# The square of the decay in the second half of a recurrent branch: on GpSimd instead of a second ScalarE exponential

## The chip, the cores and the metric

The kernel runs on one core of a Trainium2 chip. The metric is the device time of one launch in microseconds (us); three runs of the kernel before have a median of 1281.16 us. Engines are named as in the profile: PE (TensorE; PEld its weight loads), DVE (VectorE), ACT (ScalarE), POOL (GpSimd), SP (SyncE, which issues the DMAs here).

## The reference, cut to what matters

A two-layer backbone for 128 prompt and 256 sample tokens. In each layer a latent attention and a bidirectional linear recurrence (the branch) run side by side, are merged by gates, and a feed-forward block follows. The change touches the coefficients of the recurrence, which the reference computes for each of the 1024 channels in both directions as

```python
r = sigmoid(block_diag(x, w_rg) + b_rg)
i = sigmoid(block_diag(x, w_ig) + b_ig)
log_a = -8.0 * softplus(-lam) * r
a = exp(log_a)
u = sqrt(-expm1(2.0 * log_a)) * i * x
# h[t] = a[t] * h[t-1] + u[t]
```

The kernel takes sqrt(1 - a^2) as the square root of (1 + a^2) * tanh(-log_a).

## The kernel before, in words

All 384 tokens lie along the free dimension; 1024 channels are eight chunks of 128 partitions. A tile of one chunk is 128x384 in float32. Every large weight matrix comes in as loads of 128x1024 (`raw`, three buffers); ACT copies each to a rounded "high" half (`highs`, L1269) and DVE subtracts it to make the "low" half (`lows`, L1651); PE then does three products for each pair (L718 high with high, L725 high with low activations, L726 low with high). Five buffers of each half exist. The order of all work on each engine is written out by hand, and semaphores count the steps.

Each layer starts with jobs `lx0`, `lx1`, `qk`, `kr`, `gg0`, `gg1`, `m2a`, `m2b`, `m1a`, `m1b`: each is 1024x512 of weights, eight chunk steps of about 2.08 us on PE. While PE does `m2a` and `m2b`, ACT and DVE do the second group of the branch's coefficients (chunks 4 to 7, `b == 1`).

On ACT that is `lru_coefficients(1, ...)`: a table load, then for each (chunk c, direction d) one exponential of twice the argument into the scratch tile `t[d]` (L1445) and one in place for the decay `a` into `r_` (L1446). From the third pair on, the first of them waits for the DVE to be done with `t[d]`. After both directions of the next chunk are begun, `tau` of a chunk gets its logarithm (L1452) and exponential of half (L1454), both 128x768; the logarithm waits for the second direction's `squared_roots`. `highs` of the loads m2a 3, m2b 0, 1, 2 and 3 are woven in, and behind m2b 1 two reciprocal roots of the latent norms (L1360, L1363), which free the banks that `m2b` needs.

On DVE the order is: `squared_roots(4)` (L1960, `tau = (t + 1) * tau`, one 128x384 operation for each direction, each waiting for `a`), `lows` m2a 3, `squared_roots(5)`, `mod_result(6)` (small; only in layer 0), `scans(4)` (two products L1935, four scans L1939 and L1943, two tiny copies, a sum L1949), `lows` m2b 0, `squared_roots(6)`, `lows` m2b 1, `scans(5)`, `squared_roots(7)`, `lows` m2b 2, five products for the latents (L2038, L2042), `scans(6)`, `lows` m2b 3, then `lows` m1a 0, `scans(7)`.

On GpSimd, behind some memsets, the only work of a layer is the copies of rotated keys (L647, 32x512) and queries (L652, 32x128), the first of which waits for the step `cache` much later in the layer.

Of the kernel before, what the change touches and what calls it, by code (L numbers as in the profile page):

```python
# [23 lines left out]
C = D // P  # L24
# [12 lines left out]
ALU = mybir.AluOpType  # L37
ACT = mybir.ActivationFunctionType
# [166 lines left out]
def program(nc, A, plan):  # L205
# [3 lines left out]
    with ExitStack() as ctx:  # L209
        def sb(name, shape, dt=F):  # L210
            return ctx.enter_context(nc.sbuf_tensor(name, shape, dt))
# [59 lines left out]
        decay, ndecay, ndecay2 = lam[4], lam[5], lam[6]  # L271
# [5 lines left out]
        t = [sb(f"t{i}", [P, T]) for i in range(2)]  # L277
# [6 lines left out]
        def region(name, at, shape, dt=F):  # L284
            return nc.alloc_sbuf_tensor_at(name, shape, dt, offset=arena_at + at)
# [8 lines left out]
        r_ = region("lru_r", 12 * TB, [P, 2, 4, T])  # L294
# [36 lines left out]
        def qt(h):  # L331

            return qkv[:, h, :] if h < 6 else q_last[:, h - 6, :]

        def lru_under(h):

            return (keys_at + (h + 1) * TK * 4 - 1) // TB - 36
# [18 lines left out]
        PE, AC, VE, GP = tensor_done, scalar_done, vector_done, gpsimd_done  # L356
# [12 lines left out]
        def in_layer(l):  # L369


            def at(s, *label, prev=False):
                return s.sem, s.value(l - 1 if prev else l, *label)
            return at

        def last(l, s):

            return s.sem, s.count
# [29 lines left out]
        for name, reads in jobs:  # L408
            if name in HOSTED:
                reads.append((VE, "partial", HOSTED[name]))  # L410
            for r in [r for r, _, fold_job in MODS if fold_job == name]:
                reads.append((VE, "mod", r))
# [9 lines left out]
        def bank(job, b):  # L422
            return ps[4 * set_of[job] + b]
# [204 lines left out]
        @block.gpsimd  # L628
        def _(gp):
            nc.gpsimd.memset(ones[:, :], 1.0).then_inc(start_gp, 1)  # L630
            nc.gpsimd.memset(cs[:, :, :], 0.0).then_inc(start_gp, 1)
            nc.gpsimd.memset(epsc[:, 0:1], EPS).then_inc(start_gp, 1)
            nc.gpsimd.memset(epsc[:, 1:2], TINY).then_inc(start_gp, 1)
            nc.gpsimd.memset(one_row[:, 0:31], 0.0).then_inc(start_gp, 1)
            nc.gpsimd.memset(one_row[:, 31:32], 1.0).then_inc(start_gp, 1)
            nc.gpsimd.memset(one_row[:, 32:63], 0.0).then_inc(start_gp, 1)
            for s in (*raw_full, *mod_full, rows_full, gain_full, cache_full, stored):
                gp.sem_inc(s.sem, 1)
            gp.sem_inc(GP.sem, 1)
            for l in range(DEPTH):  # L640
                at = in_layer(l)
                GP.begin_layer(l)

                def key_turned(h):
                    if lru_under(h) >= 0:
                        gp.wait_ge(*at(VE, "lru_full", lru_under(h)))
                    nc.gpsimd.tensor_copy(kt[TURNED, h, :], kt[TURNED, 0, :]).then_inc(*GP.step("key_turned", h))  # L647

                def query_prompt(j):
                    gp.wait_ge(*at(AC, "qn", 3 * j + 2))  # L650
                    for e in range(4):
                        nc.gpsimd.tensor_copy(qt(4 * j + e)[TURNED, 0:TP], sq[2 + j][32 * e:32 * e + 32, 0:TP]  # L652
                                              ).then_inc(*GP.step("query_prompt", 4 * j + e))

                gp.wait_ge(*at(VE, "cache"))
                for h in range(1, 5):
                    key_turned(h)
                query_prompt(0)
                key_turned(5)
                query_prompt(1)  # L660
                key_turned(6)
                key_turned(7)
# [582 lines left out]
        def _(ac):  # L1245
# [7 lines left out]
            for l in range(DEPTH):  # L1253
                at = in_layer(l)
# [3 lines left out]
                def highs(job, i, ahead=0, layer=l):  # L1258

                    upto = layer * len(SPLIT) + SIDX[of_job(job)[i]] + ahead  # L1260
                    while made[0] <= upto:
                        lm, m = divmod(made[0], len(SPLIT))
                        n = SPLIT[m]
                        atm = in_layer(lm)
                        ac.wait_ge(*atm(raw_full[m % RAW], "load", n))

                        ac.wait_ge(*atm(PE, "used", SPLIT[m - SPL], prev=m < SPL))
                        for high, w in pieces(LOADS[n], wh[m % SPL], raw[m % RAW]):
                            nc.scalar.activation(high, w, ACT.Copy).then_inc(*AC.step())  # L1269
                        AC.also("high", n, layer=lm)  # L1270
                        made[0] += 1
# [86 lines left out]
                def inverse_root(which, src, n, dst=rstd):  # L1358

                    nc.scalar.activation(dst[:, :], src[:, 0:T], ACT.Ln, scale=1.0 / n, bias=epsc[:, 0:1]  # L1360
                                         ).then_inc(*AC.step("rs", which))
                    ac.wait_ge(*last(l, AC))
                    nc.scalar.activation(dst[:, :], dst[:, :], ACT.Exp, scale=-0.5).then_inc(*AC.step("rstd", which))  # L1363
# [68 lines left out]
                def lru_coefficients(b, after):  # L1432


                    nc.scalar.preload_act_table_set(EXP_LN)
                    ac.wait_ge(*last(l, AC))
                    order = [(j, d) for j in range(4) for d in range(2)]
                    for e in range(len(order) + 2):
                        if e < len(order):
                            j, d = order[e]  # L1440
                            c = 4 * b + j
                            k = C * d + c
                            if e >= 2:
                                ac.wait_ge(*at(VE, "squared_root", c - 1, d))
                            nc.scalar.activation(t[e % 2][:, :], r_[:, d, j, :], ACT.Exp, scale=ndecay2[:, k:k + 1]).then_inc(*AC.step())  # L1445
                            nc.scalar.activation(r_[:, d, j, :], r_[:, d, j, :], ACT.Exp, scale=ndecay[:, k:k + 1]  # L1446
                                                 ).then_inc(*AC.step("a", c, d))
                        if e >= 2 and e % 2 == 0:
                            j = e // 2 - 1
                            c = 4 * b + j  # L1450
                            ac.wait_ge(*at(VE, "squared_root", c, 1))
                            nc.scalar.activation(tau[:, :, j, :], tau[:, :, j, :], ACT.Ln, bias=epsc[:, 1:2]).then_inc(*AC.step())  # L1452
                            ac.wait_ge(*last(l, AC))
                            nc.scalar.activation(tau[:, :, j, :], tau[:, :, j, :], ACT.Exp, scale=0.5).then_inc(*AC.step("root", c))  # L1454
                        if e in after:
                            highs(*after[e])
                        if b == 0 and e in (2, 3):
                            latents(e + 2)
                        if b == 1 and e == 5:
                            ac.wait_ge(*at(PE, "latent_norms"))  # L1460
                            inverse_root("q", bank("st_qkv", 0), QL, sq[0])
                            inverse_root("kv", bank("st_qkv", 1), KVL, sq[1])

                def latents(c):

                    job, b = ("qk", c) if c < 4 else ("kr", c - 4)
                    ac.wait_ge(*at(PE, job, b))
                    if c < 5:
                        nc.scalar.activation(latent_sq[c], bank(job, b)[:, 0:T], ACT.Square).then_inc(*AC.step("sqq", c))
                    nc.scalar.activation(qkv[:, c, :], bank(job, b)[:, 0:T], ACT.Copy).then_inc(*AC.step("qkv", c))  # L1470
# [135 lines left out]
                for j in range(FC // 2):  # L1606
                    highs(f"fi{j}", -1, ahead=2)
                    for g in range(2):
                        c = 2 * j + g
# [4 lines left out]
                    for g in range(2):  # L1614
                        c = 2 * j + g
# [13 lines left out]
        def _(ve):  # L1629
# [4 lines left out]
            for l in range(DEPTH):  # L1634
                at = in_layer(l)
# [320 lines left out]

                def squared_roots(c):
                    for d in range(2):
                        ve.wait_ge(*at(AC, "a", c, d))
                        nc.vector.scalar_tensor_tensor(out=tau[:, d, c % 4, :], in0=t[d][:, :], scalar=1.0, in1=tau[:, d, c % 4, :],  # L1960
                                                       op0=ALU.add, op1=ALU.mult).then_inc(*VE.step("squared_root", c, d))

# [245 lines left out]
                for j in range(FC // 2):  # L2208
                    lows(f"fi{j}", -1, ahead=2)
                    for g in range(2):  # L2210
                        c = 2 * j + g
# [5 lines left out]
                    for g in range(2):  # L2217
                        c = 2 * j + g
# [71 lines left out]
```

## Time and profile before

| | |
|---|---|
| median of three runs (lowest, highest) | 1281.16 us (1281.06, 1282.22) |
| the profiled execution | 1280.97 us, of which the span is 1278.9 us |
| TensorE's mean granted clock | 0.997 of full speed |
| PE busy | 1242.3 us |
| DVE busy | 836.5 us |
| ACT busy | 658.0 us |
| POOL busy | 18.4 us |

The span runs from the first to the last instruction of the trace. A busy share is over the whole span and says little of a short stretch; the timeline of one engine lists its instructions with their start, duration and, in brackets, the idle time before them and what ended it. Neighbouring instructions of an engine overlap by some 0.1 us in it.

### The profile page before, as it was taken

The numbers are of one execution on the slowest core, as the hardware profiler recorded it, in microseconds if no ns is written. First come the engines' busy times: TensorE is split into PE (matmuls) and PEld (weight loads), VectorE is DVE, ScalarE is ACT, GpSimd is POOL, SyncE is SP. The second block draws the span as 40 slices with busy tenths as digits, with TensorE's granted clock in tenths as the row PEclk, the third lists the DMA queues.
The fourth block names the chain that finished last, engine by engine and source line by source line (L and its number), as shares of the span: only waits on it lengthen the run. The fifth ranks groups of instructions, "written<-read, shape, count | busy, mean of one in ns | idle before, by whom it ended". The sixth has DMA issues, their size and how long they took to land.

```text
span 1278.9 us, 19550 instructions
## 1 busy us (share of the span) xinstructions
PE 1242.3 (97%) x7457; PEld 1145.8 (90%) x7457; DVE 836.5 (65%) x1382; ACT 658.0 (51%) x1161; POOL 18.4 (1%) x41
## 2 busy tenths in 40 slices
PE   6999999999999999999999999999999999999998
PEld 4899999978879999998879998998798899999886
DVE  2697684764868877749768795756566884343423
ACT  5479873754454333342255989557445533333322
POOL 0000000200000000000000000011000000000000
PEclk9999999999999999999999999999999999999999
DMA  9645555333346766548824334263325464444451
GB/s 335 211 135 160 184 163 196 106 116 115 113 134 213 230 208 220 166 135 274 271 63 139 103 108 116 84 232 115 100 76 164 154 201 129 132 132 132 157 165 49
DMA packets 132128, 199.34 MB, mean 156 GB/s; under 512 B 10330, under 2 KB 70980, under 8 KB 132036
## 3 DMA queue, kind: packets, MB, share of 16 engines
q1 hardware_dynamic: 132036, 198.11, 48.7%
q8 instruction: 59, 0.97, 0.3%
q14 instruction: 33, 0.27, 0.1%
HBM read 196.16 MB, written 1.92 MB: 155 GB/s over the span
## 4 chain that ended last, share of the span: by engine, by line
PE 78%; DVE 10%; ACT 7%; issue 2%; DMA 1%; SPq 1%; DVEq 0%; ACTq 0%
PE bank L718 16%; PE bank L725 16%; PE bank L726 16%; PE bank L837 6%; PE bank L838 6%; PE bank L839 6%; DVE weight_low L1651 3%; ACT weight_high L1269 2%; ACT sq L1277 1%; PE bank L1137 1%; DVE lru_h L1939 1%; PE bank L1161 1%; DVE lru_tau L1943 1%; PE bank L755 1%; DVE lru_i L1935 1%
## 5 line engine op out<-in xcount | busy, mean ns | idle before, releaser
L725 PE MATMUL bank<-act_low,weight_high 128*128 128x384 f32 x1440 | 487.7, 339 | 3.6 <-DVE weight_low L1651 3.6
L726 PE MATMUL bank<-act_high,weight_low 128*128 128x384 f32 x1440 | 482.6, 335 | 0.0
L1651 DVE TENSOR_TENSOR weight_low<-raw,weight_high 128x1024 fp32r<-128x1024 f32 (+5 forms) x282 | 319.8, 1152 | 168.8 <-ACT weight_high L1269 168.4
L1269 ACT ACTIVATE weight_high<-raw 128x1024 fp32r<-128x1024 f32 (+5 forms) x282 | 273.0, 995 | 224.7 <-DMA raw<-in_w_ffn_out 62.5
L718 PE MATMUL bank<-act_high,weight_high 128*128 128x384 f32 x1440 | 315.1, 339 | 4.4 <-ACT sq L1360 2.7
L725 PEld LDWEIGHTS bank<-act_low,weight_high 128*128 128x128 f32 x1440 | 271.3, 188 | 10.9 <-DVE weight_low L1651 5.8
L726 PEld LDWEIGHTS bank<-act_high,weight_low 128*128 128x128 f32 x1440 | 271.3, 188 | 0.0
L718 PEld LDWEIGHTS bank<-act_high,weight_high 128*128 128x128 f32 x1440 | 253.6, 188 | 12.0 <-issue 4.7
L837 PE MATMUL bank<-weight_high,hid_high 128*128 128x512 f32 x264 | 103.2, 391 | 0.0
L839 PE MATMUL bank<-weight_high,hid_low 128*128 128x512 f32 x264 | 102.8, 389 | 0.0
L838 PE MATMUL bank<-weight_low,hid_high 128*128 128x512 f32 x264 | 102.8, 389 | 0.0
L1613 ACT ACTIVATE sq<-bank 128x384 f32<-128x384 f32 x44 | 19.2, 489 | 141.1 <-PE bank L726 141.1
L2215 DVE TENSOR_TENSOR t<-bank,sq 128x384 f32<-128x384 f32 x44 | 24.5, 558 | 97.2 <-PE bank L726 93.7
L837 PEld LDWEIGHTS bank<-weight_high,hid_high 128*128 128x128 f32 x264 | 49.6, 188 | 10.9 <-issue 0.6
L839 PEld LDWEIGHTS bank<-weight_high,hid_low 128*128 128x128 f32 x264 | 49.5, 188 | 10.3
L838 PEld LDWEIGHTS bank<-weight_low,hid_high 128*128 128x128 f32 x264 | 49.6, 188 | 10.1
L1675 DVE SCALAR_TENSOR_TENSOR qkv<-mod_weight,cs,qkv 128x1024 f32<-128x1024 f32 x42 | 52.0, 1279 | 1.9 <-DMA mod_weight<-in_w_mod 1.9
L1567 ACT ACTIVATE sq<-bank 128x384 f32<-128x384 f32 (+1 forms) x48 | 20.2, 421 | 55.4 <-PE bank L1146 28.2
L2156 DVE TENSOR_REDUCE negmax<-bank 128x1 f32<-128x384 f32 (+1 forms) x48 | 22.1, 464 | 31.5 <-PE bank L1137 31.3
L837 PE MATMUL bank<-weight_high,act_high 128*128 128x512 f32 x96 | 37.6, 392 | 0.0
L838 PE MATMUL bank<-weight_low,act_high 128*128 128x512 f32 x96 | 37.4, 390 | 0.0
L839 PE MATMUL bank<-weight_high,act_low 128*128 128x512 f32 x96 | 37.4, 390 | 0.0
(262 smaller groups left out, 1473.3 us busy)
## 6 DMA issues: line engine op xcount, KB each, us to landing
raw<-in_w_ffn_in SPq DMA_DIRECT2D x176, 256.0 KB, 3.9
mod_weight<-in_w_mod SPq DMA_DIRECT2D x80, 512.0 KB, 4.8
raw<-in_w_in SPq DMA_DIRECT2D x72, 512.0 KB, 4.0
raw<-in_w_ffn_out SPq DMA_DIRECT2D x44, 512.0 KB, 4.5
first_mod<-in_w_mod SPq DMA_DIRECT2D x4, 2048.0 KB, 14.2
raw<-in_w_o_lru SPq DMA_DIRECT2D x16, 512.0 KB, 3.7
raw<-in_w_out SPq DMA_DIRECT2D x16, 512.0 KB, 3.7
raw<-in_w_o_mla SPq DMA_DIRECT2D x8, 512.0 KB, 5.0
```

The costliest lines, as they stand in the source:

```text
L718: nc.tensor.matmul(bank(job, g)[:, 0:T], view[0][:, kk, cols], high[:, k, :], start=k == 0, stop=False)
L725: nc.tensor.matmul(o, view[0][:, kk, cols], low[:, k, :], start=False, stop=False)
L726: ins = nc.tensor.matmul(o, view[1][:, kk, cols], high[:, k, :], start=False, stop=k == total - 1)
L837: nc.tensor.matmul(o, high[:, k, toks], view[0][:, kk, :], start=k == 0, stop=False)
L838: nc.tensor.matmul(o, high[:, k, toks], view[1][:, kk, :], start=False, stop=False)
L839: ins = nc.tensor.matmul(o, low[:, k, toks], view[0][:, kk, :], start=False, stop=k == 2 * pairs - 1)
L1269: nc.scalar.activation(high, w, ACT.Copy).then_inc(*AC.step())
L1567: nc.scalar.activation(sq[2 + s % 2][:, 0:n * P], bank("attn", 2)[:, 0:n * P], ACT.Copy).then_inc(*AC.step("pt", s))
L1651: nc.vector.tensor_tensor(low, w, high.bitcast(F), ALU.subtract).then_inc(*VE.step())
L1675: nc.vector.scalar_tensor_tensor(out=total(r, g), in0=w, scalar=c, in1=total(r, g), op0=ALU.mult, op1=ALU.add).then_inc(*VE.step())
L2156: nc.vector.tensor_reduce(negmax[:, s % 2:s % 2 + 1], bank("attn", s % 2)[:, 0:n], AX.X, ALU.max, negate=True).then_inc(*VE.step("max", s))
L2215: nc.vector.tensor_tensor(t[c % 2][:, :], bank(f"fi{j}", 2 + g)[:, 0:T], sq[c % 4][:, :], ALU.mult).then_inc(*VE.step("hid", c))
```

## The change

For chunks 4 to 7 the exponential of twice the argument (L1445) is no longer issued on ACT, and with it goes ACT's wait for `squared_root` of the chunk before. GpSimd computes `t[d] = a * a` instead: one 128x384 product, both inputs the same tile of `r_`, for each chunk and direction, eight for a layer. It waits for `a` and, from chunk 5 on, for the DVE's reading of `t[d]` of the chunk before. DVE's `squared_roots` waits for GpSimd's product in place of ACT's `a`. The new loop stands ahead of GpSimd's key copies. Chunks 0 to 3 are as before.

```diff
@@ gpsimd, ahead of the wait for "cache"
+                for c in range(4, C):
+                    for d in range(2):
+                        if c > 4:
+                            gp.wait_ge(*at(VE, "squared_root", c - 1, d))
+                        gp.wait_ge(*at(AC, "a", c, d))
+                        nc.gpsimd.tensor_tensor(t[d][:, :], r_[:, d, c % 4, :], r_[:, d, c % 4, :], ALU.mult
+                                                ).then_inc(*GP.step("squared", c, d))
@@ scalar, lru_coefficients
-                            if e >= 2:
-                                ac.wait_ge(*at(VE, "squared_root", c - 1, d))
-                            nc.scalar.activation(t[e % 2][:, :], r_[:, d, j, :], ACT.Exp, scale=ndecay2[:, k:k + 1]).then_inc(*AC.step())
+                            if b == 0:
+                                if e >= 2:
+                                    ac.wait_ge(*at(VE, "squared_root", c - 1, d))
+                                nc.scalar.activation(t[e % 2][:, :], r_[:, d, j, :], ACT.Exp, scale=ndecay2[:, k:k + 1]).then_inc(*AC.step())
@@ vector, squared_roots
-                        ve.wait_ge(*at(AC, "a", c, d))
+                        ve.wait_ge(*(at(AC, "a", c, d) if c < 4 else at(GP, "squared", c, d)))
```

## Rows read from the trace of the kernel before

**Rows 1.** The page: busy time of PE, and the chain that ended last by engine.
```profile
PE 1242.3 (97%) x7457; PEld 1145.8 (90%) x7457; DVE 836.5 (65%) x1382; ACT 658.0 (51%) x1161; POOL 18.4 (1%) x41
...
PE 78%; DVE 10%; ACT 7%; issue 2%; DMA 1%; SPq 1%; DVEq 0%; ACTq 0%
```

**Rows 2.** Timeline of PE: end of m2a and job m2b of layer 0, then m2b of layer 1.
```profile
166.51 0.34 PE L725 MATMUL bank<-act_low,weight_high 128*128 128x384 f32 x1
...
170.45 0.97 PE L718 MATMUL bank<-act_high,weight_high 128*128 128x384 f32 x4 [0.30 <-ACT sq L1360]
...
179.58 0.33 PE L725 MATMUL bank<-act_low,weight_high 128*128 128x384 f32 x1
...
185.01 0.44 PE L725 MATMUL bank<-act_low,weight_high 128*128 128x384 f32 x1 [1.11 <-DVE weight_low L1651]
...
811.18 0.44 PE L725 MATMUL bank<-act_low,weight_high 128*128 128x384 f32 x1 [0.65 <-DVE weight_low L1651]
```

**Rows 3.** Busy time by stretch, layer 0 and 1: PE, PEld, DVE, ACT, POOL, clock, DMA.
```profile
163.30:185.00 21.70, 20.30 (x141) 19.22 (x139) 21.34 (x47) 18.82 (x28) 0.00 (x0) 1.00 0.47 141
...
789.90:811.20 21.30, 18.25 (x105) 17.61 (x103) 20.97 (x42) 18.82 (x28) 0.00 (x0) 1.00 0.29 84
```

**Rows 4.** Timeline of DVE, the second group of layer 0.
```profile
158.63 0.56 DVE L1960 SCALAR_TENSOR_TENSOR lru_tau<-t,lru_tau 128x384 f32<-128x384 f32 x1 [0.46 <-ACT lru_r L1446]
159.58 1.23 DVE L1651 TENSOR_TENSOR weight_low<-raw,weight_high 128x1024 fp32r<-128x1024 f32 x1 [0.39 <-ACT weight_high L1269]
...
163.31 0.56 DVE L1960 SCALAR_TENSOR_TENSOR lru_tau<-t,lru_tau 128x384 f32<-128x384 f32 x1 [2.04 <-ACT lru_r L1446]
163.79 0.38 DVE L1714 TENSOR_REDUCE mod<-bank 128x2 f32<-128x8 f32 x4
164.20 0.17 DVE L1718 TENSOR_TENSOR mod<-mod,par 128x8 f32<-128x8 f32 x1
...
176.12 1.22 DVE L1651 TENSOR_TENSOR weight_low<-raw,weight_high 128x1024 fp32r<-128x1024 f32 x1
...
183.74 1.22 DVE L1651 TENSOR_TENSOR weight_low<-raw,weight_high 128x1024 fp32r<-128x1024 f32 x1
```

**Rows 5.** Timeline of ACT, the same stretch.
```profile
156.46 0.62 ACT L1445 ACTIVATE t<-lru_r,lam 128x384 f32<-128x384 f32 x1
156.99 0.60 ACT L1446 ACTIVATE lru_r<-lru_r,lam 128x384 f32<-128x384 f32 x1
...
160.47 0.93 ACT L1452 ACTIVATE lru_tau<-lru_tau,epsc 128x768 f32<-128x768 f32 x1
...
162.18 0.60 ACT L1445 ACTIVATE t<-lru_r,lam 128x384 f32<-128x384 f32 x1
162.68 0.60 ACT L1446 ACTIVATE lru_r<-lru_r,lam 128x384 f32<-128x384 f32 x1
163.19 1.05 ACT L1269 ACTIVATE weight_high<-raw 128x1024 fp32r<-128x1024 f32 x1
```

**Rows 6.** Timeline of POOL, layer 0: key and query copies.
```profile
207.68 0.60 POOL L647 COPY keys<-keys 32x512 f32<-32x512 f32 x1 [206.27 <-DVE keys L2080]
...
235.06 0.88 POOL L647 COPY keys<-keys 32x512 f32<-32x512 f32 x1 [2.45 <-DVE t L2118]
...
243.28 0.84 POOL L652 COPY q_last<-sq 32x128 f32<-32x128 f32 x2
```

**Rows 7.** Timeline of DVE around those copies.
```profile
234.91 0.55 DVE L2100 TENSOR_TENSOR act_low<-t,act_high 128x384 fp32r<-128x384 f32 x1
235.38 1.10 DVE L1651 TENSOR_TENSOR weight_low<-raw,weight_high 128x512 fp32r<-128x512 f32 x1
236.41 0.68 DVE L1651 TENSOR_TENSOR weight_low<-raw,weight_high 128x512 fp32r<-128x512 f32 x1
...
242.66 1.76 DVE L2113 TENSOR_TENSOR qkv<-sq 32x256 f32<-32x256 f32 x4
```

## The prediction

> **What bounds the kernel now.** I read the page first: PE is busy 97% of the span and holds 78% of the chain that ended last; DVE has 10% and ACT 7% of it [rows 1]. So a change on ACT, DVE and POOL moves the time only where PE waits for them. The timeline of PE over the second group of coefficients shows where: in job m2b of layer 0 PE stands 1.11 us, and in layer 1 0.65 us, until the low half of the last load, m2b 3, is made by DVE [rows 2]. Behind these two points PE runs on, so what this low half gains or loses is the gain or loss of the layer. The 0.30 us at the start of m2b, which ACT ends, is no bound of its own: PE would only reach the later stall sooner.
>
> The timeline of DVE says what sets that low half. It starts at 183.74; DVE last stood idle for long (2.04 us) before the second L1960 of chunk 5, at 163.31, waiting for ACT's decay [rows 4]. From there on it is busy 21.34 of 21.70 us in layer 0 and 20.97 of 21.30 us in layer 1 [rows 3]. So the time at which PE goes on is: the start of that L1960, plus the DVE work behind it, plus whatever disturbs DVE on the way. ACT, which the change relieves, matters up to 163.3 and then no more; POOL, which it loads, is empty in both stretches (0.00) [rows 3].
>
> **What is removed.** Eight exponentials of 0.60 us, which lie about 0.51 us apart, for a layer [rows 5]: 4.1 us of ACT. Four of them stand ahead of the decay that DVE awaits at 163.31 (chunk 4 and 5, both directions): 4 x 0.51 = 2.0 us at most. The other four come while DVE is the bound and are worth nothing. ACT's wait for `squared_root` goes too; the logarithm L1452 keeps its own, on the second direction of the same chunk.
>
> **What is added, the product itself.** The trace shows no two-input operation on POOL. The nearest row is its 32x512 copy: 0.60 us undisturbed [rows 6]. How long it keeps the memory reads shows from a collision, below: 0.42 us for 512 elements, 0.82 ns each, so about 0.2 us of the copy is fixed. For 384 elements one pass is 0.32 us, two (both inputs one after the other) are 0.64, three (and the write) are 0.96. Bounds for the hold H: 0.32 to 0.96 us. I take 0.80, between two and three passes, since a product has one input more than the copy and must write as well. The product lasts G = H + 0.2 = 1.0 us (0.5 to 1.16). GPSIMD Engine Reference of the Trainium skill (3.1, elementwise cycle accounting) gives 4497 ns for a two-input operation of 2048 elements, 2.2 ns an element, an estimate of 0.84 us for H; the sum below would come out 0.6 us higher.
>
> **What is added, the collision.** At 235.06 POOL starts a copy while DVE runs L2100 (234.91 to 235.46). The copy takes 0.88 in place of 0.60 us: it waits. The next DVE instruction, L1651 at 235.38, takes 1.10 us where the one behind it, of the same shape, takes 0.68: it waits 0.42 [rows 6, 7]. So the two shut each other out instruction by instruction, and a POOL operation that is waiting gets in ahead of DVE's next. Four L2113 at 242.66 fit this: they span 1.76 us instead of 1.44 (0.42 each, 0.34 apart), 0.11 us more for each step, which is what 128 elements cost at 0.82 ns [rows 7]. SBUF — State Buffer of the Trainium skill (Who interferes with whom) says that a DVE instruction with two SBUF inputs and a GpSimd one that reads SBUF block each other fully; by that rule, too, the products cost DVE their whole hold, and the collision at 235.4 agrees.
>
> Nearly everything DVE does in the bound run has two SBUF inputs: L1651, L1935, L1960, the scans, L1949, L2038. So a product that falls into it costs DVE about H, though POOL itself has nothing else to do.
>
> **The start of the run, step by step (layer 0).** The first decay is now where the first exponential was: out at 156.46 + 0.62 = 157.1. Products 4,0 and 4,1 follow: 157.1 + G, then H + 0.1 more, 159.0 (case G = 1.0). DVE is shut out or behind, so both its L1960 of chunk 4 come after: 0.05 + 0.47 + 0.56, done at 160.1, where they were done at 159.2 [rows 4]. L1452 waits for that; from its start to the end of the decay of (5,1) were 160.47 to 163.28 us with an exponential of 0.51 in between, so 2.3 us now [rows 5]: 162.4. Then product 5,1: 0.05 + G, and 0.05 to DVE: 163.5, against 163.31. In H: 161.14 + 3H, that is 163.54 at 0.80 and 163.06 and 164.02 at 0.64 and 0.96. Three products in series eat the 2 us of ACT: **+0.2 us** (-0.3 to +0.7). Waiting behind these on DVE is everything, low halves included, but that of m2a 3 ends at 160.8 and PE wants it at 166.51, 5.7 us later [rows 2, 4]. Layer 1 repeats these steps without a difference that matters. DMAs, SP and the key copies of POOL (207.7) are far behind and touch nothing.
>
> **The four products inside the run** (chunks 6 and 7). Product 6,0 needs its decay, out on ACT about 163.9 (162.4, then a high half of 1.0 and itself 0.5 [rows 5]); DVE then has 5,1 behind it. In layer 0 it meets the small reductions from PSUM (163.79 to 164.2, one input), which hide about 0.4 us [rows 4]; layer 1 has none. Product 6,1 falls in scans(4), 7,0 behind the first L1960 of chunk 6, 7,1 in scans(5). Each waits for one DVE instruction and then holds the next back by H. There is no idle time of DVE to take them in: 21.70 - 21.34 us is 0.4, all of it short gaps.
>
> Layer 0: 0.2 + 4 x 0.8 - 0.4 = +3.0. Layer 1: 0.2 + 3.2 = +3.4. What is late next: low m2b 2 would end at 177.3 + 3 = 180.3, and PE wants it at 179.58 [rows 2, 4], so PE stands there first and then again at m2b 3; the sum stays that of the last. ACT's relief (rs earlier, the 0.30 us gone) only makes PE arrive at the stall sooner. PE then has no slack later that would take it back, as job follows job and it is the bound. Profiled 1280.97 + 6.4 = **1287.4 us**; the median before lies 0.2 above the profiled execution, inside the precision of this sum. With H of 0.64 the sum is 4.2 (1285.2), with 0.96 it is 8.7 (1289.7).
>
> **Rivals.**
> A. No shutting out that matters (DVE wins the port in its gaps, or a square of one tile reads cheaply). Then only the start moves: 157.7 + 2G + 2.4 + G = 160.1 + 3G, against 163.31. With G = 1.0 that is -0.2 us a layer: 1280.6, no change. For it: POOL copies of 128 elements pass beside DVE with 0.11 us each. Against it: the 0.42 us at 235.38.
> B. The same with a fast product, G = 0.52 (one pass): 161.7, -1.6 us a layer, 1277.7. This is the other side, faster, and its turning point is G = 1.07 without collisions. With collisions and one pass the start gains 1.2 and four holds of 0.32 give it back: -0.3 and +0.1 us, 1280.7.
> C. The scans do not shut POOL out (no row shows the two beside each other): products 6,1 and 7,1 are free, 1.6 us less a layer: 1284.2.
> D. A price at the first product of a kind on POOL. The first key copy takes 0.60 us like the others [rows 6], which speaks against it; if there were 6 us at 157.1 in layer 0, DVE would start its run that much later: 1293. The GPSIMD Engine Reference (2.1, dispatch) names about 6 us for the first call to freshly loaded code, and no row here shows one.
>
> **How the numbers follow.** Forecast 0.57 (1285.2 to 1289.7). C 0.16. A, with the one-pass variant with collisions, 0.16. B 0.05. D or other double costs 0.06. Range: 1280.2 takes in A and C; 1290.5 is the forecast's end with some room; B and D stay out. A measurement of this kernel can tell about 0.2% (2.6 us) from no change. Faster by more: B, 0.05. Within: A and a third of a C with smaller holds, 0.20. Slower: the forecast, most of C, and D, 0.75.
>
> **What would show it.** Right: POOL products of 0.9 to 1.4 us, the longer ones where they wait; DVE instructions beside them 0.6 to 0.9 us longer than their kind; the second L1960 of chunk 5 still near 163.3 to 164; low m2b 3 at about 186.7 and PE's stall before it near 3 to 4 us in all, with one at m2b 2. Wrong: DVE's forms as long as before and a start at 161 to 163 (A, B); only L1935, L1949 and L1651 stretched and the scans not (C); a long gap before the first product (D). If PE's later stalls shrink by what these grow, the bound was misread.

## The result and the profile after

The changed kernel takes 1289.68 us in the median (1287.17 to 1290.4, five runs), the kernel before beside it 1282.22 us: 1.0061 times as long, 95% interval 1.005 to 1.0072. A second set of five runs on another chip gave 1288.74 against 1280.79 us, 1.0065 (1.0052 to 1.0077). The profiled execution took 1287.17 us, 6.2 us more than that of before; its span is 1285.4 us, 6.5 us more. Two single runs of experiments, of 4754.6 and 5834.21 us, are left out of the medians below.

The page of the changed kernel, its busy line:

```profile
PE 1246.1 (97%) x7457; PEld 1149.4 (89%) x7457; DVE 843.7 (66%) x1382; ACT 650.8 (51%) x1145; POOL 33.4 (3%) x57
```

Against [rows 1], ACT has 16 instructions and 7.2 us less, POOL 16 instructions and 15.0 us more; and DVE, whose instructions are the same 1382, is busy 7.2 us longer. PE's stalls in m2b, which answer to [rows 2]:

```profile
180.99 0.44 PE L732 MATMUL bank<-act_low,weight_high 128*128 128x384 f32 x1 [0.16 <-DVE weight_low L1659]
188.61 0.45 PE L732 MATMUL bank<-act_low,weight_high 128*128 128x384 f32 x1 [3.17 <-DVE weight_low L1659]
...
807.84 0.45 PE L732 MATMUL bank<-act_low,weight_high 128*128 128x384 f32 x1 [0.53 <-DVE weight_low L1659]
815.46 0.69 PE L732 MATMUL bank<-act_low,weight_high 128*128 128x384 f32 x1 [3.18 <-DVE weight_low L1659]
```

PE now stands 3.17 and 3.18 us where it stood 1.11 and 0.65 (the load m2b 3), and shortly once more one load earlier (m2b 2), as the prediction had it. (The lines of code moved: L1651 is L1659, L1960 is L1968, L1935 is L1943, L1939 and L1943 are L1947 and L1951, L1949 is L1957, L1446 is L1454, L1435 is L1442, L725 is L732, L1718 is L1726.) DVE over the same stretch of layer 0, answering to [rows 4]:

```profile
159.65 1.63 DVE L1968 SCALAR_TENSOR_TENSOR lru_tau<-t,lru_tau 128x384 f32<-128x384 f32 x2 [1.89 <-POOL t L660]
...
162.97 0.55 DVE L1968 SCALAR_TENSOR_TENSOR lru_tau<-t,lru_tau 128x384 f32<-128x384 f32 x1
164.64 0.56 DVE L1968 SCALAR_TENSOR_TENSOR lru_tau<-t,lru_tau 128x384 f32<-128x384 f32 x1 [1.12 <-POOL t L660]
165.12 0.38 DVE L1722 TENSOR_REDUCE mod<-bank 128x2 f32<-128x8 f32 x4
165.53 0.72 DVE L1726 TENSOR_TENSOR mod<-mod,par 128x8 f32<-128x8 f32 x1
...
168.21 0.98 DVE L1951 TENSOR_TENSOR_SCAN lru_tau<-lru_r,lru_i 128x128 f32<-128x128 f32 x1
...
172.67 1.85 DVE L1659 TENSOR_TENSOR weight_low<-raw,weight_high 128x1024 fp32r<-128x1024 f32 x1
...
175.49 0.93 DVE L1947 TENSOR_TENSOR_SCAN lru_h<-lru_r,lru_i 128x128 f32<-128x128 f32 x1
```

And POOL beside it:

```profile
163.78 0.83 POOL L660 TENSOR_TENSOR t<-lru_r 128x384 f32<-128x384 f32 x1 [1.81 <-ACT lru_r L1454]
165.40 0.83 POOL L660 TENSOR_TENSOR t<-lru_r 128x384 f32<-128x384 f32 x1 [0.79 <-DVE mod L1722]
167.70 1.22 POOL L660 TENSOR_TENSOR t<-lru_r 128x384 f32<-128x384 f32 x1 [1.47 <-DVE lru_h L1947]
172.36 1.07 POOL L660 TENSOR_TENSOR t<-lru_r 128x384 f32<-128x384 f32 x1 [3.45 <-DVE lru_tau L1968]
175.25 0.89 POOL L660 TENSOR_TENSOR t<-lru_r 128x384 f32<-128x384 f32 x1 [1.81 <-ACT lru_r L1454]
```

An undisturbed product takes 0.83 us. The last four of a layer lie in DVE's run, and each has one stretched DVE instruction beside it: L1726 0.72 in place of 0.17 us, a scan of 128 elements 0.98 in place of 0.40, L1659 1.85 in place of 1.22, a scan 0.93 in place of 0.42. That is 0.55 + 0.58 + 0.63 + 0.51 = 2.27 us. In layer 1 the same four products lengthen these:

```profile
792.35 1.65 DVE L1943 TENSOR_TENSOR lru_i<-lru_i,lru_tau 128x384 f32<-128x384 f32 x2
...
795.02 1.03 DVE L1951 TENSOR_TENSOR_SCAN lru_tau<-lru_r,lru_i 128x128 f32<-128x128 f32 x1
...
799.52 1.85 DVE L1659 TENSOR_TENSOR weight_low<-raw,weight_high 128x1024 fp32r<-128x1024 f32 x1
...
802.34 0.93 DVE L1947 TENSOR_TENSOR_SCAN lru_h<-lru_r,lru_i 128x128 f32<-128x128 f32 x1
```

Against 1.02, 0.40, 1.22 and 0.42 us in the kernel before that is 0.63 + 0.63 + 0.63 + 0.51 = 2.40 us.

To compare kernels without what happens elsewhere in an execution, I read one length in each trace and layer: from ACT's table load that opens the second group to the instant at which PE goes on with m2b 3. In the kernel before these table loads are

```profile
155.17 1.28 ACT L1435 ACT_TABLE_LOAD   x1
...
781.77 1.28 ACT L1435 ACT_TABLE_LOAD   x1
```

so with 185.01 and 811.18 [rows 2] the lengths are 29.84 and 29.41 us. In the changed kernel:

```profile
156.80 1.28 ACT L1442 ACT_TABLE_LOAD   x1
...
784.02 1.28 ACT L1442 ACT_TABLE_LOAD   x1
```

31.81 and 31.44 us: +1.97 and +2.03. The start of DVE's run moved from 8.14 to 7.84 us behind the table load (163.31 - 155.17, 164.64 - 156.80), -0.30; with the 2.27 us of stretched instructions that makes the 1.97 of layer 0. In layer 1 it moved by as much (789.92 - 781.77 is 8.15, 791.87 - 784.02 is 7.85), and 2.40 - 0.30 is 2.10 against 2.03 measured.

Both layers together give 4.0 us, but the kernel is 6 to 8 us slower. A part of the rest is in the granted clock. These are stretches of layer 1 in and behind the stall (PE, PEld, DVE, ACT, POOL busy, the clock, DMA):

```profile
812.00:815.00 3.00, 0.28 (x2) 0.00 (x0) 2.93 (x7) 1.34 (x3) 0.00 (x0) 1.00 0.00 0
815.00:818.00 3.00, 2.54 (x8) 2.54 (x9) 2.97 (x6) 0.00 (x0) 0.00 (x0) 0.51 0.45 106
818.00:821.00 3.00, 3.00 (x18) 3.00 (x17) 2.31 (x6) 0.59 (x2) 0.00 (x0) 0.92 0.71 245
```

After 3.18 us without a matmul PE runs at 0.51 (1.2 in place of 2.4 GHz), which costs at most 0.49 x 3 + 0.08 x 3 = 1.7 us; some 0.2 us of that fall in the last 0.46 us of the stall, where PE still stood. Behind the 3.17 us of layer 0 the clock stayed at 1.00 in this execution. The mean granted clock of the five runs is 0.991 to 0.994, that of before's profile 0.997, and the two runs at 0.994 (1287.17, 1287.83) are about 2 us shorter than the three at 0.991 and 0.992. The runs of before beside the experiments lie between 0.994 and 0.999.

The stall of layer 1 did not grow by lateness alone. The start of m2b there, before and after:

```profile
797.06 0.98 PE L718 MATMUL bank<-act_high,weight_high 128*128 128x384 f32 x4 [2.40 <-ACT sq L1360]
...
797.29 0.97 PE L725 MATMUL bank<-act_high,weight_high 128*128 128x384 f32 x4 [0.38 <-ACT sq L1367]
```

Before, PE stood 2.40 us here for ACT and the granted clock stayed at 1.00. With ACT relieved it stands 0.38 us, and a part of the idle time moves to the one stall at m2b 3: from 0.65 to 3.18 us, and 0.53 at m2b 2, where the low half came 2.03 us later.

### The profile page after: what moved, and what is told of

Read it like the earlier page. It is cut to its first block, busy times and chain, and to the rows that moved or that the text cites. A ratio compares the mean times of both kernels' runs of the same rounds, so it can differ in the third digit from the quotient of the medians.

```text
span 1285.4 us, 19564 instructions
## 1 busy us (share of the span) xinstructions
PE 1246.1 (97%) x7457; PEld 1149.4 (89%) x7457; DVE 843.7 (66%) x1382; ACT 650.8 (51%) x1145; POOL 33.4 (3%) x57
## 3 DMA queue, kind: packets, MB, share of 16 engines
HBM read 196.16 MB, written 1.92 MB: 154 GB/s over the span
## 4 chain that ended last, share of the span: by engine, by line
PE 79%; DVE 10%; ACT 5%; issue 2%; DMA 2%; SPq 0%; DVEq 0%; POOL 0%; ACTq 0%
PE bank L725 17%; PE bank L732 16%; PE bank L733 16%; PE bank L844 5%; PE bank L845 5%; PE bank L846 5%; DVE weight_low L1659 3%; ACT weight_high L1276 1%; PE bank L1144 1%; DVE lru_h L1947 1%; PE bank L1168 1%; PE bank L762 1%; ACT sq L1284 1%; DVE lru_tau L1951 1%; DVE lru_i L1943 1%
## 5 line engine op out<-in xcount | busy, mean ns | idle before, releaser
L732 PE MATMUL bank<-act_low,weight_high 128*128 128x384 f32 x1440 | 489.1, 340 | 9.4 <-DVE weight_low L1659 9.4
L1659 DVE TENSOR_TENSOR weight_low<-raw,weight_high 128x1024 fp32r<-128x1024 f32 (+5 forms) x282 | 322.2, 1161 | 171.0 <-ACT weight_high L1276 170.5
L725 PE MATMUL bank<-act_high,weight_high 128*128 128x384 f32 x1440 | 315.6, 339 | 2.0 <-ACT act_high L1361 1.2
L732 PEld LDWEIGHTS bank<-act_low,weight_high 128*128 128x128 f32 x1440 | 272.2, 189 | 17.3 <-DVE weight_low L1659 12.2
L725 PEld LDWEIGHTS bank<-act_high,weight_high 128*128 128x128 f32 x1440 | 254.5, 189 | 9.2 <-issue 3.9
```

The costliest lines, as they stand in the source:

```text
L725: nc.tensor.matmul(bank(job, g)[:, 0:T], view[0][:, kk, cols], high[:, k, :], start=k == 0, stop=False)
L732: nc.tensor.matmul(o, view[0][:, kk, cols], low[:, k, :], start=False, stop=False)
L1659: nc.vector.tensor_tensor(low, w, high.bitcast(F), ALU.subtract).then_inc(*VE.step())
```

## The experiments

Each ran beside the kernel before on the same chip. Theory 1: a GpSimd product that reads memory and a VectorE instruction shut each other out, and what lengthens the run is these holds. Theory 2, the rival: the loss is VectorE waiting at its semaphores for slow products.

**Products beside, unused.** The kernel before, with the eight products added into a free tile that nobody waits for before the region is reused. Cut from the excerpt: GpSimd first waits until the tile is free, and ACT waits for the last product behind its wait for the scans of chunk 7.

```diff
+                for c in range(4, C):
+                    for d in range(2):
+                        if c > 4:
+                            gp.wait_ge(*at(VE, "squared_root", c - 1, d))
+                        gp.wait_ge(*at(AC, "a", c, d))
+                        gp.wait_ge(GP.sem, GP.count)
+                        nc.gpsimd.tensor_tensor(rstd[:, :], r_[:, d, c % 4, :], r_[:, d, c % 4, :], ALU.mult
+                                                ).then_inc(*GP.step("squared", c, d))
```

> The kernel before, unchanged on ScalarE and VectorE, with the eight GpSimd products of each layer added beside it; they write a spare tile that nobody reads. Theory 1 (each product that reads memory shuts VectorE out for its hold, 0.63 us as the changed kernel's trace shows, and the reverse): the run of VectorE ends later by 4 to 5 holds in each layer, 2 to 3 us, so 4 to 6 us in all, 1286 to 1288 us, though nothing waits for GpSimd. Theory 2 (the loss of the changed kernel is VectorE's waiting for slow products at its semaphores): no change, within 1 us.

Measured: 1287.67 against 1281.39 us, 1.0052 (1.0039 to 1.0065). The lengths are 32.19 and 32.18 us, +2.35 and +2.77. DVE in layer 0 (here L1946 is L1935 of before, L1950 and L1954 are L1939 and L1943, L1960 is L1949):

```profile
164.19 0.38 DVE L1729 TENSOR_TENSOR mod<-mod,par 128x8 f32<-128x8 f32 x1
...
165.54 0.93 DVE L1950 TENSOR_TENSOR_SCAN lru_h<-lru_r,lru_i 128x128 f32<-128x128 f32 x1
...
168.35 0.96 DVE L1960 TENSOR_TENSOR lru_h<-lru_h,lru_tau 128x384 f32<-128x384 f32 x1
...
172.45 1.65 DVE L1946 TENSOR_TENSOR lru_i<-lru_i,lru_tau 128x384 f32<-128x384 f32 x2
...
175.12 0.98 DVE L1954 TENSOR_TENSOR_SCAN lru_tau<-lru_r,lru_i 128x128 f32<-128x128 f32 x1
```

DVE never waits for these products, and the loss is as large as with the change. The run starts where it did (163.30 against 163.31), and, ACT not being relieved, five products fall into it: 0.21 + 0.51 + 0.40 + 0.63 + 0.58 = 2.33 us of stretched instructions, against +2.35 measured. Theory 2 falls.

**No square at all.**

```diff
-                        nc.vector.scalar_tensor_tensor(out=tau[:, d, c % 4, :], in0=t[d][:, :], scalar=1.0, in1=tau[:, d, c % 4, :],
+                        nc.vector.scalar_tensor_tensor(out=tau[:, d, c % 4, :], in0=t[d][:, :] if c < 4 else r_[:, d, c % 4, :], scalar=1.0, in1=tau[:, d, c % 4, :],
```

with the GpSimd loop left out and ACT as in the change.

> The second group without any square: ScalarE issues only the eight decays, GpSimd does nothing, VectorE reads the decay itself where it read the square. Left out of the computation: the square in chunks 4 to 7. This is the relief of ScalarE alone. Worked out from the timeline: the second VectorE L1960 of chunk 5 starts at 161.3 in place of 163.3, so 2.0 us less in each layer, 4 us in all, 1278 us. A theory by which VectorE is the bound all along and ScalarE's relief is worth nothing gives no change.

Measured: 1275.12 against 1281.39 us, 0.9954 (0.9942 to 0.9967). In layer 1 PE goes on at 805.84, 27.32 us behind the table load at 778.52: -2.09, as the timeline of before gave. In layer 0 PE does not stand at m2b 3 at all: it starts that product at 183.29, 27.92 us behind the table load at 155.37 (-1.92), and the low half was ready at 183.13. So ACT's relief is worth about 2 us a layer when the square is free, 4.0 us in all. The other 2 us of the difference are not in this stretch.

**Chunks 4 and 5 alone, chunks 6 and 7 alone.** In the three places of the change:

```diff
-                for c in range(4, C):
+                for c in range(4, 6):
...
-                            if b == 0:
+                            if not 4 <= c < 6:
...
-                        ve.wait_ge(*(at(AC, "a", c, d) if c < 4 else at(GP, "squared", c, d)))
+                        ve.wait_ge(*(at(AC, "a", c, d) if not 4 <= c < 6 else at(GP, "squared", c, d)))
```

and the same with 6 and 8.

> The change for chunks 4 and 5 alone; 6 and 7 keep ScalarE's second exponential. Theory 1: the run of VectorE starts 0.3 us sooner in each layer and no product falls into it: 0 to 1 us less than before. Theory 2 (waiting for products): chunks 4 and 5 are the ones whose products VectorE waits for, so here is the whole loss, 6 us more than before.

> The change for chunks 6 and 7 alone; 4 and 5 keep ScalarE's second exponential. Theory 1: four products shut VectorE out for 0.63 us each in its bound run, less some 0.4 us in layer 0: 2.1 and 2.5 us, 4.6 us more in all, and perhaps 1 to 2 us on top where a longer stall of TensorE is followed by a stretch at the lower clock. Theory 2: VectorE never waits for these products, so no change.

Measured for 4 and 5: 1280.79 against 1281.39 us, 0.9995 (0.9986 to 1.0004), lengths 29.55 and 29.05, -0.29 and -0.36. For 6 and 7: 1287.66 us, 1.0043 (1.0031 to 1.0056), lengths 32.08 and 31.21, +2.24 and +1.80. The products of chunks 4 and 5, which DVE waits for, cost nothing; those of chunks 6 and 7 are the whole loss. Layer 1 came out 0.7 us under the 2.5 expected, and the timeline of DVE there shows where from:

```profile
794.49 1.25 DVE L1947 TENSOR_TENSOR_SCAN lru_h<-lru_r,par,lru_i 128x256 f32<-128x256 f32 x1
...
796.73 0.15 DVE L1954 COPY hst<-lru_h 128x1 f32<-128x1 f32 x1
796.80 0.14 DVE L1955 COPY hst<-lru_tau 128x1 f32<-128x1 f32 x1
796.98 0.76 DVE L1957 TENSOR_TENSOR lru_h<-lru_h,lru_tau 128x384 f32<-128x384 f32 x1
```

One product fell beside the two tiny copies, which have one input each, and held back the sum behind them by 0.20 us only (L1957, 0.76 for 0.56); the other three cost 0.5 to 0.6 us each.

**One input in place of two.**

```diff
-                        nc.gpsimd.tensor_tensor(t[d][:, :], r_[:, d, c % 4, :], r_[:, d, c % 4, :], ALU.mult
+                        nc.gpsimd.tensor_copy(t[d][:, :], r_[:, d, c % 4, :]
```

> The changed kernel with a GpSimd copy of the decay, one input, in place of the product, in all eight places; left out of the computation: the square in chunks 4 to 7. If the hold goes by passes over the memory (0.82 ns an element and input), GpSimd's instruction is 0.52 us, VectorE's stretched instructions are 0.32 us longer and not 0.63, the start of the run comes 1.2 us earlier than before the change, and the layer is even: within 1 us of before. If each GpSimd instruction has a fixed price whatever it reads, it is as slow as the changed kernel.

Measured: 1282.33 against 1280.79 us, 1.001 (0.9997 to 1.0023); lengths 29.27 and 29.20, -0.57 and -0.21. POOL and DVE in layer 1:

```profile
789.58 0.51 POOL L660 COPY t<-lru_r 128x384 f32<-128x384 f32 x1 [0.98 <-ACT lru_r L1454]
...
790.60 1.35 DVE L1943 TENSOR_TENSOR lru_i<-lru_i,lru_tau 128x384 f32<-128x384 f32 x2
...
793.28 1.01 DVE L1951 TENSOR_TENSOR_SCAN lru_tau<-lru_r,par,lru_i 128x256 f32<-128x256 f32 x1
...
797.13 1.52 DVE L1659 TENSOR_TENSOR weight_low<-raw,weight_high 128x1024 fp32r<-128x1024 f32 x1
```

The copy takes 0.51 us and stretches DVE by 0.33 (1.35 for 1.02), 0.29 (1.01 for 0.72) and 0.30 (1.52 for 1.22): half of the product's 0.63. The fourth of this layer costs 0.20 (0.93 for 0.73). So the hold fits one price for each input read, about 0.32 us for 384 elements; a copy and a product differ in the operation too, and no run holds the two apart.

**The changed kernel again, and TensorE kept busy in its stall.** Theory 3: the idle stretch costs a second time through the lower clock. Theory 4: these falls come by chance.

```diff
                             if kk == 0:
+                                if job == "m2b" and i == 3:
+                                    for f in range(24):
+                                        nc.tensor.matmul(bank(job, f % 4)[:, T:512], ident[:, :], ident[:, :], start=False, stop=False,
+                                                         skip_group_check=True)
                                 pe.wait_ge(*at(VE, "low", n))
```

> The changed kernel once more, on the chip of the three runs beside it: 6 to 9 us more than before. In its first profile TensorE's stall of 3.18 us in layer 1 was followed by some 3.4 us at half of the granted clock, the one of 3.17 us in layer 0 was not; where both are, it is nearer to 9, where none, to 5.

> The changed kernel with 24 small matmuls on TensorE (identity with identity, into unused columns of the same banks) ahead of the wait for the last low half of m2b; they fill some 2.6 us of the 3.2 us stall and nobody reads them. Theory 3 (the idle stretch costs a second time, by the lower clock that follows it): the granted clock stays full behind the stall in both layers and the kernel is 1.7 to 3.4 us faster than the changed one, 4 to 5 us above before. Theory 4 (the clock's falls come by chance and owe nothing to this stall): the same time as the changed kernel, and a fall there as often as in it.

Measured: the changed kernel 1288.74 us, 8.0 us over before, with a fall of the clock at both stalls of its profiled execution; with 24 small matmuls 1289.25 us: no difference, as theory 4 says. But the timeline of PE shows why:

```profile
185.39 5.52 PE L729 MATMUL bank<-ident 128*128 128x128 f32 x48
190.67 0.42 PE L736 MATMUL bank<-act_low,weight_high 128*128 128x384 f32 x1
```

They took 5.5 us, not 2.6 (I had counted half of them: each is two in the trace), and the layer was 1.8 us longer than the changed kernel's, 190.67 - 157.08 = 33.59. The clock had not fallen at m2b in either layer, so one price may hide the other. Half as many tell them apart:

> As the run with 24 small matmuls, with 12 of them: the 24 took 5.5 us, 2 us more than the stall, and the fall of the granted clock was absent in both layers, so one hid the other. Theory 3: 12 take 2.8 us, fit in the 3.2 us, and the kernel is 1.7 to 3.4 us faster than the changed kernel, 1285 to 1287 us. Theory 4: it stays where the changed kernel is, 1289 us.

```profile
183.80 2.73 PE L729 MATMUL bank<-ident 128*128 128x128 f32 x23
187.04 0.44 PE L736 MATMUL bank<-act_low,weight_high 128*128 128x384 f32 x1 [0.51 <-DVE weight_low L1663]
```

```profile
812.00:815.00 3.00, 3.00 (x27) 3.00 (x26) 2.93 (x8) 1.76 (x4) 0.00 (x0) 1.00 0.00 0
815.00:818.00 3.00, 2.50 (x16) 2.31 (x15) 2.97 (x5) 0.00 (x0) 0.00 (x0) 1.00 0.34 55
```

Measured: 1285.88 against 1281.15 us, 1.0036 (1.0022 to 1.005), where the changed kernel had 1.0061 and 1.0065. The small matmuls take 2.7 us (the rows above leave out the first of 24). The lengths are the changed kernel's, 31.80 and 31.45, and the clock stays at 1.00. So about 3 us of the loss is the clock at the two stalls (3.2 and 3.7 us by the two ratios of the changed kernel; the intervals, 1.005 to 1.0072 and 1.0052 to 1.0077, lie just above that of this run). Over all traces with a stall of 2.8 to 3.2 us there, the clock fell at 9 of 11 stalls, in eight of them up to 1.2 us before PE went on, once 0.7 us behind; with the small matmuls at 0 of 4. The two exceptions are layer 0 of the first profile and the 3.10 us of layer 1 in the run with one input.

**All products on VectorE.**

```diff
+                    if c >= 4:
+                        for d in range(2):
+                            if c > 4:
+                                ve.wait_ge(*at(VE, "squared_root", c - 1, d))
+                            ve.wait_ge(*at(AC, "a", c, d))
+                            nc.vector.tensor_tensor(t[d][:, :], r_[:, d, c % 4, :], r_[:, d, c % 4, :], ALU.mult).then_inc(*VE.step())
                     for d in range(2):
```

> The changed kernel with all eight products of a layer on VectorE itself, in pairs, GpSimd left out. Each costs VectorE about 0.47 us of its own time, less than the 0.63 us for which a GpSimd product shuts it out. The start of the run comes 0.8 us earlier, four products in it cost 1.9 us: 1.1 us more in each layer, 2 to 3 us in all over before, so 3 to 6 us less than the changed kernel. If GpSimd's products were partly hidden, this would be slower than the changed kernel.

Measured: 1284.65 against 1281.15 us (12 runs), 1.0029 (1.0014 to 1.0043); lengths 30.92 and 30.41, +1.08 and +1.00, as worked out. DVE is better off doing the product itself (0.47 us) than being shut out by GpSimd (0.63 us), and the interval lies below both of the changed kernel.

**The order of ScalarE alone, and with the products of chunks 4 and 5 on VectorE.** Both take the decay of (5, second direction) together with the first:

```diff
-                        if e < len(order):
-                            j, d = order[e]
+                        for j, d in ([] if (b, e) == (1, 3) else order[e:e + (2 if (b, e) == (1, 2) else 1)]):
```

> The kernel before with ScalarE's order alone changed: both exponentials of (5, second direction) ahead of the logarithm of chunk 4. The second L1960 of chunk 5 then runs 1.7 us sooner, but the scans of chunk 4 wait for the root, which ends at 163.2: 1.0 us earlier in layer 0 and 0.5 us in layer 1, 1.5 us less than before in all.

> Products of chunks 4 and 5 on VectorE, in pairs, where it stood idle before the run; chunks 6 and 7 keep ScalarE's second exponential; ScalarE takes the decay of (5, second direction) ahead of the logarithm of chunk 4; nothing on GpSimd. By the timeline VectorE's run then starts at 162.2 in place of 163.9, 1.6 us earlier in each layer, and no product lies in it: 3.2 us less than before, 1278 us. If the start of the run is not what sets the layer, no change.

Order alone: 1279.87 against 1281.15 us, 0.999 (0.998 to 1.0001); lengths 29.41 and 29.42, -0.43 and 0.0: less than expected, and not told from no change. The scans of chunk 4 did start 0.9 us (165.19 - 156.97 against 164.29 - 155.17) and 0.4 us sooner behind the table load, but DVE then stood 0.37 and 0.38 us before the low half of m2b 2 (L1650 at 177.48 and 803.95) until ACT had made the high half, and lost the gain again but for those 0.4 us of layer 0. With the products on DVE (`4 <= c < 6` in the diff above): 1275.65 us (1275.19 to 1277.9), 0.9963 (0.9948 to 0.9977), better than both kernels. DVE in layer 0:

```profile
157.27 1.06 DVE L1963 TENSOR_TENSOR t<-lru_r 128x384 f32<-128x384 f32 x2 [0.98 <-ACT lru_r L1446]
158.25 1.02 DVE L1968 SCALAR_TENSOR_TENSOR lru_tau<-t,lru_tau 128x384 f32<-128x384 f32 x2
159.19 1.22 DVE L1651 TENSOR_TENSOR weight_low<-raw,weight_high 128x1024 fp32r<-128x1024 f32 x1
160.32 1.02 DVE L1963 TENSOR_TENSOR t<-lru_r 128x384 f32<-128x384 f32 x2
161.26 1.02 DVE L1968 SCALAR_TENSOR_TENSOR lru_tau<-t,lru_tau 128x384 f32<-128x384 f32 x2
162.20 0.38 DVE L1714 TENSOR_REDUCE mod<-bank 128x2 f32<-128x8 f32 x4
```

The idle 2.04 us of before are filled with products, and the reductions start at 162.20 in place of 163.79. The lengths are 28.86 and 27.60, -0.98 and -1.81, 2.8 us together. Layer 0 starts its run 1.74 us sooner behind the table load but gains less, since DVE waits there later for ACT:

```profile
175.28 1.23 DVE L1651 TENSOR_TENSOR weight_low<-raw,weight_high 128x1024 fp32r<-128x1024 f32 x1 [0.39 <-ACT weight_high L1269]
```

The 5.5 us measured are more than the 2.8; the rest is not shown by the lengths.

## Why the prediction was right, point by point

**The bound.** Right: the end of the low half of m2b 3 sets each layer. Every kernel that moved it by more than 1 us moved the time the same way; the four exponentials that ACT no longer does in chunks 6 and 7 were worth nothing (without any square the start moved by 2.04 us in layer 1 and the length by 2.09). That the 0.30 us for which ACT held PE at the start of m2b is no bound was right too, but the prediction gave the value of layer 0 alone; in layer 1 it was 2.40.

**Start of the run.** The step gave 161.14 + 3H (its own terms add up to 161.08, which changes nothing), +0.2 us at H = 0.80. It measured -0.30 in both layers, and at the measured H of 0.63 the same formula gives 163.0, or -0.3. The chain of three products in series, collisions included, was read rightly; its size was off by that of H.

**The hold H.** This is the term that was mis-sized: 0.63 us, where 0.80 was taken; the low value, two passes, was the right one. I had added a price for writing; the runs with a copy (0.32) and a product (0.63) need none. The whole product is 0.83 us, not 1.0. SBUF — State Buffer of the Trainium skill (Who interferes with whom) says that two such instructions contend and that the shared port pair is an exclusive lock; the traces agree in kind, with a hold of 0.63 us of a product of 0.83. The estimate from the GPSIMD Engine Reference of the Trainium skill (3.1, elementwise cycle accounting), 0.84 us, fits the whole instruction and not its hold.

**The four products in the run.** Right in number, place and direction: 6,0 at the small reductions, 6,1 and 7,1 in scans, 7,0 behind L1968 of chunk 6. The scans are shut out like the others (0.58, 0.51), so rival C falls; A falls with them, though its start of the run (-0.2) is near the measured one, by luck of G: at the measured 0.83 us its formula gives -0.7; B needed a product of 0.52 us without holds, and there were holds; D did not appear, the first two products took 1.61 us together, as long as later ones. Where I had 0.4 us hidden by the reductions of layer 0, only 0.1 was: L1726 behind them has two inputs and was held back 0.55 us.

**What the sum left out.** With H = 0.63 the sum is 4.1 us (4.4 with 0.1 hidden in place of 0.4), and the two lengths give 4.0. That the forecast of 6.4 was met by 6.2 in the profiled execution is luck: a second price, the lower clock at a longer stall, was missing from it and took the place of what H had too much. In that execution it was paid once at m2b (1.5 us with PE at work), and the clock fell once more elsewhere than in before's profile; 4.0 + 1.5 + 1.7 is 7.2 us where the span grew by 6.5, so 0.7 us is not placed. The prediction named the stall and its length (3 to 4 us in all, in fact 3.3 and 3.7 a layer) but put at nothing that a stall of such length may slow the work behind it. About 3 us in the median are due to it: the median loss is 7.5 and 8.0 us in the two sets.

**What stays open.** Falls of the clock also come elsewhere: in the profile of before two (at 376 and 664), in that of the changed kernel three beside the one at 815 (44, 665 and 1003), in that of the best kernel none before the end of the work. They are not free of stalls either. Each begins within 2 us behind a shorter one, of 1.18 us (PE goes on at 42.90 in the changed kernel) or 1.8 us (PE goes on at 374.41 and 661.84 before, at 1002.09 after). But every kernel stands in these places for 1.1 to 1.8 us, and over the 13 traces the clock fell at 26 of the 39 near 376, 664 and 1003. At up to 1.7 us each, such falls are of the size of what the lengths leave over (about 2.7 us for the best kernel, about 2 for the one with no square). What decides whether a stall brings one about, and whether the edits at 160 us have anything to do with the one at 376 us, was not tried.

## What to carry to other kernels

An idle engine is no free engine if its instructions and those of the engine that sets the time shut each other out: ask, for each instruction moved to GpSimd, what VectorE does in that very microsecond, and price it at the hold (here 0.63 us a product) and not at zero. A helper's work belongs where the bound engine waits anyway; here that was the same 2 us in which VectorE could do it itself. And a stall on TensorE that grows to some 3 us may be paid twice (9 of 11 here), so look at the granted clock around it.

## What was not expected of the hardware

A 128x384 product on GpSimd with both inputs the same tile took 0.83 us undisturbed. Where it fell into VectorE's run it lengthened one instruction by 0.51 to 0.63 us, whether that was a 128x8 sum, a scan, a 128x384 product or a 128x1024 subtraction; by 0.20 to 0.40 us where a part of it met short one-input instructions. A one-input copy of the same shape lengthened one by 0.33 us at most.

TensorE's clock fell to its lower level at 9 of 11 stalls of 2.8 to 3.2 us in one and the same place. Six of these falls lasted about 3.4 us and three about 6.8 us. 12 small matmuls in the stall, whose results nobody reads, made the changed kernel 3 us faster.
